# Weight chunks of a fused MLP prepared one step earlier, pair sums and accumulator turns moved to other jobs

## The reference

```python
u = rms_norm(h, norm_mlp_g)
h = h + square(relu(u @ w_mlp1)) @ w_mlp2      # (512,1024) @ (1024,4096), (512,4096) @ (4096,1024)
x = rms_norm(h, final_norm_g)                  # then the second block, whose first product is x_norm @ w_in_2
```

## Time and profile before

| | |
|---|---|
| median of 3 runs | 1370.11 us (1369.26 to 1372.03) |
| the profiled execution's own time | 1373.74 us |
| its span, first to last instruction | 1372.0 us |
| mean granted TensorE clock | 0.993 of full |
| PE busy | 1333.9 us (97%) |
| DVE busy | 1048.0 us (76%) |
| ACT busy | 626.0 us (46%) |
| POOL busy | 61.2 us (4%) |
| DMA | 130.33 MB at 95 GB/s |

### The profile page before, as it was taken

The page is one execution under the profiler, slowest core; times in us unless marked ns, Lnnn a source line. Parts: engine busy times, 40 slices in busy tenths (PEclk is TensorE's granted clock), DMA queues, the critical chain, the costliest instruction groups (busy, mean ns, idle before and its releaser), DMA issues.

```text
span 1372.0 us, 17133 instructions
## 1 busy us (share of the span) xinstructions
PE 1333.9 (97%) x6357; PEld 1087.8 (79%) x6357; DVE 1048.0 (76%) x1715; ACT 626.0 (46%) x1076; POOL 61.2 (4%) x60
## 2 busy tenths in 40 slices
PE   7999999999999899899898999999999999999998
PEld 6787777788888688687777778878888888888886
DVE  7868888885667856867875674598899888995685
ACT  7535565564554454434332453743343434343234
POOL 1000000102011000000000410000000000000000
PEclk9999999999999999999999999999999999999999
DMA  5333333233333243333332233232232223223232
GB/s 161 92 92 77 78 76 94 78 113 117 93 92 91 86 131 107 108 92 115 100 100 70 77 100 115 77 96 81 82 109 80 79 84 97 77 82 107 85 115 92
DMA packets 204340, 130.33 MB, mean 95 GB/s; under 512 B 21426, under 2 KB 190467, under 8 KB 204258
## 3 DMA queue, kind: packets, MB, share of 16 engines
q1 hardware_dynamic: 202642, 126.62, 31.7%
q10 hardware_dynamic: 1616, 2.62, 0.6%
HBM read 127.12 MB, written 2.10 MB: 94 GB/s over the span
## 4 chain that ended last, share of the span: by engine, by line
PE 83%; DVE 10%; ACT 4%; issue 2%; ACTq 0%; DVEq 0%
PE lin L752 20%; PE lin L756 19%; PE lin L755 19%; DVE wl L1962 2%; PE ob L1255 1%; PE sc L844 1%; ACT wh L1414 1%; PE sc L1112 1%; PE sc L1108 1%; PE sc L1111 1%; PE tr L1108 1%; PE tr L1111 1%; PE sc L1211 1%; PE tr L1112 1%; PE sc L1214 1%
## 5 line engine op out<-in xcount | busy, mean ns | idle before, releaser
L1962 DVE TENSOR_TENSOR wl<-raw,wh 128x1024 fp32r<-128x1024 f32 (+2 forms) x211 | 259.7, 1232 | 76.3 <-ACT wh L1414 75.4
L752 PE MATMUL lin<-uh,wh 128*128 128x512 f32 x624 | 251.9, 404 | 3.1 <-DVE acc L2471 1.9
L1414 ACT ACTIVATE wh<-raw 128x1024 fp32r<-128x1024 f32 (+2 forms) x211 | 214.4, 1018 | 87.1 <-DMA raw<-in_w_mlp_dram 17.0
L756 PE MATMUL lin<-uh,wl 128*128 128x512 f32 x624 | 244.1, 391 | 0.0
L755 PE MATMUL lin<-ul,wh 128*128 128x512 f32 x624 | 243.9, 391 | 0.0
L752 PE MATMUL lin<-vh,wh 128*128 128x512 f32 x512 | 202.6, 396 | 0.2 <-DVE te L2692 0.2
L755 PE MATMUL lin<-vl,wh 128*128 128x512 f32 x512 | 199.6, 390 | 0.0
L756 PE MATMUL lin<-vh,wl 128*128 128x512 f32 x512 | 199.3, 389 | 0.0
L752 PEld LDWEIGHTS lin<-uh,wh 128*128 128x128 f32 x624 | 117.8, 189 | 31.1 <-issue 3.8
L755 PEld LDWEIGHTS lin<-ul,wh 128*128 128x128 f32 x624 | 117.9, 189 | 24.9 <-issue 2.2
L756 PEld LDWEIGHTS lin<-uh,wl 128*128 128x128 f32 x624 | 117.6, 188 | 25.0
(11 more groups left out here) (666 smaller groups left out, 2501.6 us busy)
## 6 DMA issues: line engine op xcount, KB each, us to landing
raw<-in_w_in_dram SPq DMA_DIRECT2D x100, 512.0 KB, 3.8
raw<-in_w_mlp_dram SPq DMA_DIRECT2D x64, 512.0 KB, 3.9
raw<-in_w_out_dram SPq DMA_DIRECT2D x16, 512.0 KB, 3.5
raw<-in_w_xkv_dram SPq DMA_DIRECT2D x8, 512.0 KB, 3.5
raw<-in_w_proj_b_dram SPq DMA_DIRECT2D x8, 512.0 KB, 3.7
raw<-in_w_proj_a_dram SPq DMA_DIRECT2D x8, 512.0 KB, 3.6
raw<-in_w_mlp_dram SPq DMA_DIRECT2D x12, 256.0 KB, 2.6
xtok<-in_x_dram ACTq DMA_DIRECT2D x4, 512.0 KB, 5.1
```

Source lines behind the costliest of these rows:

```text
L752: ins = pe.matmul(o, wh[:, slot, at], xh_, start=start, stop=False)
L756: return pe.matmul(o, wl[:, slot, at], xh_, start=False, stop=stop)
L1414: act.activation(wh[:, c.slot(4), 0:size], raw[:, c.slot(2), 0:size], ACT.Copy).then_inc(hi_made, 1)
L1962: dve.tensor_tensor(wl[:, c.slot(4), 0:size], raw[:, c.slot(2), 0:size], wh[:, c.slot(4), 0:size].bitcast(F32), ALU.subtract).then_inc(lo_ ...
```

## The change

Seven things are changed, and no instruction is added or taken away:

1. In `up0` to `up2`, ACT splits and DVE lowers chunk c+m+3 in the pass of job m (pass 0 does c+2 and c+3). In `up3` both stay at c+m+2.
2. Two pair sums move: in quarters 1 and 2 pair 0 goes from pass 5 to pass 3 and pair 1 from pass 6 to pass 5. In quarter 0 pair 0 goes ahead of the lowering in pass 5.
3. In quarters 1 and 2 the first two loads of `down` are issued in the middle of the up loads (behind u5).
4. In `seven` DVE lowers v3 ahead of `sums_low(u, 3)` and `pair_sums(u, 2)`.
5. In `down3` ACT splits chunk c+m+3 in pass m, while DVE still lowers c+m+2.
6. In `down3` DVE makes the low half of tile m-1 instead of tile m in pass m.
7. PE's waits for the combined totals go from the start of jobs 2 and 6 of `up3` into `turn_acc(0)` and `turn_acc(4)`, in the middle of those jobs. Turns 0 to 5 lie in jobs 2 to 7, at row tile 4, and turns 6 and 7 in job 0 of `down3`. Before, turns 4 to 7 lay two each in jobs 6 and 7.

```diff
 # SP: seven_loaded(u, r) issues load r of down{u}, as the loop did before
             for q in range(4):
                 ...
                     load(c + m, a["w_mlp1"][0], q * FFQ + P * m, DT, P)
+                    if 0 < q < SEVENS and m == 5:
+                        for r in range(2):
+                            sp.wait_ge(lo_made, seven_lowered(q - 1, 8 + r))
+                            sp.wait_ge(sums_made, seven_sum(q - 1, r, 4))
+                            seven_loaded(q, r)
 ...
 # PE
             def turn_acc(f):
 
+                if f % 4 == 0:
+                    taken(SEVENS - 1, SEVEN_PARTS + (16 if f else 8))
                 if f > 1:
                     pe.wait_ge(h_added, f - 1)
 ...
-                    if q == SEVENS and m in (2, 6):
-                        taken(SEVENS - 1, SEVEN_PARTS + (8 if m == 2 else 16))
                     job(c + m, j + m, DT, uh, ul, before=...,
-                        between=turns(m) if q == SEVENS else {})
+                        between={4: lambda f=m - 2: turn_acc(f)} if q == SEVENS and m > 1 else {})
 ...
             c, j = phase("down3")
             for m in range(DT):
-                job(c + m, j + m, DT, fh, fl, before=...)
+                job(c + m, j + m, DT, fh, fl, before=...,
+                    between={2: lambda: turn_acc(DT - 2), 5: lambda: turn_acc(DT - 1)} if m == 0 else {})
 # ACT, up
-                    split(c + (m + 2))
-                    if q < SEVENS and m == 7:
-                        split(c + 10)
+                    if q == SEVENS or m == 0:
+                        split(c + (m + 2))
+                    if q < SEVENS:
+                        split(c + (m + 3))
                     to(j + m, (ta, tb)[m % 2][:], ACT.Relu)
 # ACT, down3
-                    split(c + (m + 2))
+                    if m == 0:
+                        split(c + 2)
+                    if m < DT - 1:
+                        split(c + (m + 3))
                     act.wait_ge(h_added, DT + m + 1)
 # DVE, up
-                    lower(c + (m + 2))
-                    if q < SEVENS and m == 5:
+                    if q == SEVENS or m == 0:
+                        lower(c + (m + 2))
+                    if q == 0 and m == 5:
                         pair_sums(q, 0)
-                    if q < SEVENS and m == 6:
+                    if q < SEVENS:
+                        lower(c + (m + 3))
+                    if 0 < q < SEVENS and m == 3:
+                        pair_sums(q, 0)
+                    if q < SEVENS and m == (5 if q else 6):
                         pair_sums(q, 1)
-                    if q < SEVENS and m == 7:
-                        lower(c + 10)
 ...
-                    if q == SEVENS and 1 < m < 6:
+                    if q == SEVENS and m > 1:
                         turned_added(m - 2)
-                    if q == SEVENS and m > 5:
-                        turned_added(2 * m - 8)
-                        turned_added(2 * m - 7)
 # DVE, seven(u)
+                lower(c + 3)
                 sums_low(u, 3)
                 pair_sums(u, 2)
-                lower(c + 3)
                 lower(c + 4)
 # DVE, down3
             for m in range(DT):
+                if m == 0:
+                    turned_added(DT - 2)
+                    turned_added(DT - 1)
                 lower(c + (m + 2))
 ...
                 dve.tensor_tensor(at, part_[:], at, ALU.add).then_inc(h_added, 1)
-                gain_low(ul[:, m, :], at, both[:, m:m + 1], uh[:, m, :], U0["raw"] + m + 1)
+                if m:
+                    gain_low(ul[:, m - 1, :], h[:, m - 1, :], both[:, m - 1:m], uh[:, m - 1, :], U0["raw"] + m)
+            gain_low(ul[:, DT - 1, :], h[:, DT - 1, :], both[:, DT - 1:DT], uh[:, DT - 1, :], U0["raw"] + DT)
```

More of the change, by code:

```diff
@@ L611, in _, with seven_loaded @@
             stream("xo", a["w_xo"][0], 0, 4, 256)
+            def seven_loaded(u, r):
+                kk, odd = (r // 2, r % 2) if r < 8 else (r - 8, 1)
+                first, n = (512, 512) if r < 8 and odd else (0, 1024)
+                row = u * FFQ + (2 * kk + odd) * P
+                sp.dma_start(RAW_SLOTS[r % 4][:, 0:n], a["w_mlp2"][0][row:row + P, first:first + n])\
+                    .then_inc(SLOT_LANDED[r % 4], 16)
             for q in range(4):
@@ L623, in _ @@
                     continue
-                for r in range(SEVEN_LOADS):
+                for r in range(2 if q else 0, SEVEN_LOADS):
                     if r < 2:
[L626 to L630, removed]
+                        sp.wait_ge(std_made, NORM_NO["mlp"] + 1)
                     elif r < 4:
@@ L1176, in turn_acc @@
                 ins.then_inc(part_ready, 1)
[L1178 to L1183, removed]
             for q in range(4):
@@ L1199, in _ @@
             for m in range(DT):
-                job(c + m, j + m, DT, fh, fl, before=tiles_of(f_low, 12 * SEVENS) if m == 0 else None)
+                job(c + m, j + m, DT, fh, fl, before=tiles_of(f_low, 12 * SEVENS) if m == 0 else None,
+                    between={2: lambda: turn_acc(DT - 2), 5: lambda: turn_acc(DT - 1)} if m == 0 else {})
             def token_products(c, m, q, ready):
```

## The result

| | before | after |
|---|---|---|
| median of 4 runs each, same chip | 1371.07 us (1369.26 to 1373.66) | 1355.76 us (1354.08 to 1356.16) |
| ratio | | 0.9885, 95% interval 0.9865 to 0.9904 |
| span of the profiled execution | 1372.0 us | 1354.0 us |
| its mean granted TensorE clock | 0.993 | 0.996 |

The change wins 15.3 us between the medians (13.2 to 18.5 by the interval) and 18.0 us between the two profiled spans. The prediction was 1353 us, with 1349 to 1359 as its range. The page counts 17136 instructions, 3 more than before. All three are semaphore events of PE, and the matmuls and the work of the other engines are the same in number.

The account below looks back on a forecast made before the run. PE was busy 97%, so only idle or slow PE could be won. Terms 1.3 + 3.0 + 3.0 + 7.7 + 3.7 = 18.7 us, less 1.5 for clock, gave 17.2: 1370.11 to 1353 us, range 1349 to 1359.

Parts of the forecast that it names:

- POOL's hold: In `down3`, POOL's sums could block DVE's two-input instructions, 1.3 us twice a pass, making DVE's pass 5.7 us at most.
- Edit 7: In `up3`, waits for totals (2.2 us) and job 7's excess (5.9) go, 0.4 is lost at turn 7: 7.7 us won.
- Edits 5 and 6: In `down3` and `values`, two waits each and restart delays at six matmuls go: 3.7 us won.
- One loss of the clock: Behind one of the three 2.2 us waits for v4, PE falls to its lower clock: 1.5 us lost.
- (a): v4 waits cost the clock all three times, and turn 7 or a quarter's start waits: 13 us won, 1357; chance 0.2.
- (b): DVE's heavy passes 3 and 5 keep the last ReLU late; quarters 1 and 2 win 1 us each, 1357; chance 0.1.
- (c): `down3` stays paced by POOL's hold on DVE, and its 3.7 us are not won: 1356.5; chance 0.07.
- (d): Chunk loads of 9 us hold up each of 32 jobs by 1 us: slower, 1383; chance 0.02.
- (e): DVE's total work of a quarter, not its order, sets the pace, so PE idles elsewhere: 1370; chance 0.03.

Follow-up runs that it names:

- the kernel with pair 2 first: Against the changed kernel, DVE in `seven` does pair 2's three additions first, then lowers v3 and v4, then `sums_low`: 1348.29 us, ratio to before 0.9825.
- the kernel with the late reciprocal: Against the kernel with pair 2 first, the MLP norm's 3.4 us reciprocal on DVE goes from pass 3 of `up0` to pass 0 of `up1`: 1345.49 us.

## Why the prediction was right

**Mechanism.** Every wait that the prediction named went, and the new one stands where it put it. In `down2` the three waits were laid out, with their restarts, as 0.3, 1.3 and 2.2 us. By the distances of the matmuls they came as 0.23, 1.14 and 2.19, of which 0.97 and 2.03 are idle. The ReLU starts at 642.14, behind a split that waited for nothing. In `down0` the v3 wait vanished and v4 waits 1.83 us. Turn 7 in job 0 of `down3` waits 0.43 us for the h of turn 5. One mechanism was told too simply. "So ACT and DVE hand a pass to and fro, which takes longer than PE's 5.44 us" is true of the 6.5 us that were measured, but 1.1 us of them are POOL's hold on the lowering, as the run with edits 5 and 6 undone shows.

**Terms.** `down0` 1.2 for 1.3, `down1` 3.3 for 3.0 where the clock held (45.42 to 42.12) and 1.6 where it didn't, `down2` 3.3 for 3.0. Edit 7 measured 7.7 for 7.7 by the traces, 4.9 of it without any loss of the clock and 2.8 of clock, and 6.2 by the medians. Edits 5 and 6 measured 4.0 for 3.7. One loss of the clock in the three waits for v4 was counted. The first trace has exactly one, the second none. Over the five traces that have these waits in `down1` and `down2` it is three losses in ten, so one was a fair guess, but in a single execution it is chance. The profiled execution took 1355.72 us where 1356.5 were worked out.

**The step that was off.** It is the last one: "That lies 3.63 us over the median of the runs shown, so the median becomes 1370.11 - 17.2 = 1352.9". The 25 executions of the kernel before on four occasions have a median of 1372.2 us, between 1368.86 and 1374.58. Three runs had landed 2.1 us low, and the profiled 1373.74 lies 1.5 above the median and not 3.63. Some of the terms are losses of the clock that some executions have and some don't, so a median of three says little to within 2 us. From 1372.2 the sum gives 1355.0, and the changed kernel has 1355.7. Against the 1370.11 of the prediction only 14.4 us are left of the 17.2, and the result of 1355.76 lies just inside the forecast of 1350 to 1356.

**Rivals.** (a), the clock lost behind all three v4 waits, happened in none of the five traces that have them. (b) fell: the last ReLU is on time. (c) fell: in `down3` DVE waits for PE in every pass but the first, as the timeline of after shows, where it waited for ACT before.

```profile
757.40 0.69 DVE L2516 TENSOR_TENSOR tc<-lin,logit 128x512 f32<-128x512 f32 x1 [2.23 <-PE lin L761]
...
759.40 1.22 DVE L1965 TENSOR_TENSOR wl<-raw,wh 128x1024 fp32r<-128x1024 f32 x1
```

The text spoke of "lowerings of still up to 2.3 us" and weighed 2.6 us of POOL's hold in each pass. In `down3` that hold is gone from pass 2 on (in pass 1 POOL holds the sum into h for 0.4 us): the lowering begins ahead of POOL's first sum and takes 1.22 us, and now POOL gives way. Its first sum takes 1.59 us there, and 1.34 behind the last job, where no lowering runs beside it. The lowering of 2.35 us comes only once, behind the last job, at the same time as POOL's second sum (POOL's rows first, then DVE's):

```profile
760.18 1.59 POOL L737 TENSOR_TENSOR qt<-qt,ta 128x512 f32<-128x512 f32 x1 [2.42 <-ACT ta L1737]
...
776.50 1.34 POOL L737 TENSOR_TENSOR qt<-qt,ta 128x512 f32<-128x512 f32 x1 [2.42 <-ACT ta L1737]
777.98 1.30 POOL L737 TENSOR_TENSOR kt<-kt,tb 128x512 f32<-128x512 f32 x1
```

```profile
778.02 2.35 DVE L1965 TENSOR_TENSOR wl<-raw,wh 128x1024 fp32r<-128x1024 f32 x1 [1.34 <-ACT wh L1413]
```

Whoever began first was not held, by 0.8 us in the one case (759.40 and 760.18) and by 0.04 us in the other. The Trainium skill, SBUF — State Buffer, section Who interferes with whom, says the same: the order of issue decides which of the two is blocked. The prediction took from that section only that DVE is blocked, and so counted a hold in every pass. POOL has time to spare, 2.42 us idle ahead of its first sum, so the new order costs nothing.

(d) fell: ACT's splits do wait longer for loads of the MLP's weights than before (23.3 us in all, before 17.0), 2.7 us at most, but no wait of PE comes from it.

```profile
ACT wh L1413 <- DMA raw<-in_w_mlp_dram: 23.3, 14, 2.7
```
(e) fell: in the kernel with pair 2 first the waits for v4, which the change had left on DVE, went away by its order alone.

## What to carry to other kernels

When a wait moves from one chunk to the next, read what the late instruction's engine does ahead of it, and ask who wants that work. Here 1.4 us of sums that were needed later stood ahead of a chunk that was needed at once. Moving these sums alone behind it won only 1.6 us. Putting pair 2 in front, where DVE would have waited 1.75 us for ACT, and the sums behind, won 6.7. Put first what another engine must work on next, so that its answer is made while this engine does what it alone needs. Such an order also shows where an engine waits idle ahead of a backlog: that idle time is what a reorder can use, and the busy share doesn't show it.

Set a prediction against several executions of the kernel before. If its waits are long enough to cost the clock in some of them, its time has steps, here of 1.7 to 2.8 us.

## What the runs showed of the hardware

Whether the clock is lost does not hang on the length of the wait alone. Behind a loss the granted clock is 0.50 (568.5 to 571.9 us in the changed kernel's first trace), which is the level of 1.2 GHz, and matmuls start 0.43 us apart. An idle time of PE of 2.03 us in `down1` was followed by that in one execution of the changed kernel and not in another. Over five traces with 1.99 to 2.03 us of idle for v4 in `down1` and `down2` it came three times in ten. One idle time of 2.84 us was followed by it in the kernel before, but not in the traced execution with edit 7 undone. Both of 3.25 us with edit 4 undone were, and so was the wait for the last ReLU of `up0`, of 3.59 to 3.88 us, in all nine traces that have it. Those of 1.2 us and less in the kernel with the late reciprocal were not. The 8 executions of the kernel with the late reciprocal lie within 1.3 us of each other, the 25 of the kernel before within 5.7. What else than the length of the wait decides it stays open.
